# Latent attention in a two-block transformer kernel: units of one head and one query block, and another order of values, first queries and key rotation

## The reference, cut to what matters

```
MLA_HEADS = 8; MLA_NOPE = 64; MLA_ROPE = 32; MLA_SCALE = (64 + 32) ** -0.5; Q_BLOCK = 128

def attention(q_nope, q_rope, k_nope, k_rope, v):
    ...
    def one_block(qs):
        qn, qr = qs
        s = jnp.einsum('bqhd,bkhd->bhqk', qn, k_nope) + jnp.einsum('bqhr,bkr->bhqk', qr, k_rope)
        p = jax.nn.softmax(s.astype(jnp.float32) * MLA_SCALE, axis=-1).astype(v.dtype)
        return jnp.einsum('bhqk,bkhd->bqhd', p, v)
...
k_nope, v = mla_keys_values(kv_c, kv_norm_g, w_ukv)      # kv_c of rank 256
q_nope, q_rope = mla_queries(q_c, q_norm_g, w_uq)        # q_c of rank 384
q_rope = rope_2d(q_rope, ang_row[:, None, :], ang_col[:, None, :])
k_rope = rope_2d(k_rope, ang_row, ang_col)
```

## Time and profile before

| | |
|---|---|
| median of the runs | 3021.17 us |
| the profiled execution | 3019.46 us |
| its span, first to last instruction | 3017.7 us |
| granted TensorE clock, mean over the span | 0.969 of full speed |
| busy share of the span: TensorE, its weight loads | 94%, 75% |
| VectorE, GpSimd, ScalarE | 48%, 38%, 33% |
| DMA read | 364.04 MB, 123 GB/s over the span |

### The profile page before, as it was taken

How to read it: one execution, slowest core, us unless ns; L and a number is a source line. 1 busy time by engine, 2 the same in 40 slices (tenths; PEclk the granted TensorE clock), 3 DMA queues, 4 the chain that set the end, 5 groups by cost and what they waited for, 6 DMA issues and landing times.

```text
span 3017.7 us, 36418 instructions
## 1 busy us (share of the span) xinstructions
PE 2846.8 (94%) x12748; PEld 2261.4 (75%) x12748; DVE 1463.1 (48%) x2627; ACT 997.9 (33%) x1409; POOL 1136.1 (38%) x488
## 2 busy tenths in 40 slices
PE   7999999999999899999899999898788999999997
PEld 4888877778888788887678888787443777788886
DVE  3524365543425534255835253644454365563635
ACT  2222245332322322234532222244333453343322
POOL 2444443234444344443234444453210233344433
PEclk9999999999999999999989999899899999999998
DMA  6535432234436444353215453542100113322221
GB/s 246 209 117 181 147 146 84 79 117 168 154 124 209 138 172 151 140 180 113 70 56 183 142 188 128 193 143 77 70 28 15 56 56 147 112 84 98 97 98 42
DMA packets 69266, 374.32 MB, mean 124 GB/s; under 512 B 7776, under 2 KB 8544, under 8 KB 38656
## 3 DMA queue, kind: packets, MB, share of 16 engines
q1 hardware_dynamic: 65424, 359.61, 33.7%
q10 hardware_dynamic: 3696, 12.85, 1.1%
HBM read 364.04 MB, written 8.39 MB: 123 GB/s over the span
## 4 chain that ended last, share of the span: by engine, by line
PE 39%; issue 33%; POOL 20%; DVE 4%; ACT 2%; DVEq 1%; ACTq 1%; DMA 1%; SPq 1%; POOLq 0%
POOL w_lo L403 20%; PE psum L468 10%; PE psum L470 10%; PE psum L469 10%; PE psum L884 1%; PE psum L862 1%; PE psum L487 1%; PE psum L488 1%; PE psum L489 1%; PE psum L874 1%; DVE psum L1875 1%; PE psum L933 1%; PE psum L935 0%; PE psum L934 0%; SPq L364 0%
## 5 line engine op out<-in xcount | busy, mean ns | idle before, releaser
L403 POOL TENSOR_TENSOR w_lo<-raw,w_hi 128x1024 fp32r<-128x1024 f32 x464 | 1115.0, 2409 | 1723.7 <-ACT w_hi L953 1723.6
L468 PE MATMUL psum<-h_hi,w_hi 128*128 128x512 f32 x2112 | 833.3, 395 | 17.2 <-DVE h_lo L1394 16.6
L469 PE MATMUL psum<-h_lo,w_hi 128*128 128x512 f32 x2112 | 829.1, 393 | 0.0
L470 PE MATMUL psum<-h_hi,w_lo 128*128 128x512 f32 x2112 | 828.3, 392 | 0.0
L953 ACT CAST w_hi<-raw 128x1024 fp32r<-128x1024 f32 x464 | 482.0, 1048 | 913.8 <-PE psum L470 753.6
L468 PEld LDWEIGHTS psum<-h_hi,w_hi 128*128 128x128 f32 x2112 | 401.5, 190 | 106.9 <-DVE h_lo L1394 15.9
L469 PEld LDWEIGHTS psum<-h_lo,w_hi 128*128 128x128 f32 x2112 | 401.5, 190 | 83.8 <-issue 0.5
L470 PEld LDWEIGHTS psum<-h_hi,w_lo 128*128 128x128 f32 x2112 | 400.9, 190 | 84.6
L468 PE MATMUL psum<-hid_hi,w_hi 128*128 128x512 f32 x880 | 349.7, 397 | 4.7 <-DVE hid_lo L1881 4.7
L470 PE MATMUL psum<-hid_hi,w_lo 128*128 128x512 f32 x880 | 349.5, 397 | 0.0
L469 PE MATMUL psum<-hid_lo,w_hi 128*128 128x512 f32 x880 | 349.4, 397 | 0.0
(11 more groups left out here) (343 smaller groups left out, 3067.9 us busy)
## 6 DMA issues: line engine op xcount, KB each, us to landing
raw<-in_weights_dram SPq DMA_DIRECT2D x232, 1024.0 KB, 5.8
mod_raw<-in_mod_w_dram SPq DMA_DIRECT2D x192, 512.0 KB, 4.3
first_mods_a<-in_mod_w_dram SPq DMA_DIRECT2D x8, 512.0 KB, 12.0
first_mods_b<-in_mod_w_dram SPq DMA_DIRECT2D x8, 512.0 KB, 15.4
first_mods_a<-gate_spill ACTq DMA_DIRECT2D x4, 1024.0 KB, 10.9
gate_spill<-gate_out_c ACTq DMA_DIRECT2D x5, 512.0 KB, 3.0
x<-in_xT_dram SPq DMA_DIRECT2D x1, 2048.0 KB, 8.6
x_spill<-x ACTq DMA_DIRECT2D x1, 2048.0 KB, 11.6
```

What stands on the lines that cost most here:

```text
L403: pool.tensor_tensor(w_lo[:, k % 2, cs], raw[:, k % 4, cs], w_hi[:, k % 2, cs].bitcast(F32), ALU.subtract).then_inc(lo_ready, 1)
L468: pe.matmul(out, wh, rhs_hi[:, c, :], start=(c == ks[0]), stop=False)
L469: pe.matmul(out, wh, rhs_lo[:, c, :], start=False, stop=False)
L470: mm = pe.matmul(out, wl, rhs_hi[:, c, :], start=False, stop=(c == ks[-1]))
```

## The change

The attention becomes one loop over 32 units u (head u // 4, query block u % 4). Each unit is turned and multiplied by the values alone: six transposes into banks 4 and 5, two copies on ScalarE into one of two buffers of 768 columns (`turned`: `prod` and a new tile), six matmuls of 128 columns. VectorE scales a unit once its own exponential is there, ahead of the row maximum of the unit after it. On TensorE the order is: turn unit u, scores of unit u + 2, values of unit u - 1. Queries of the next pair are computed after the turn of the pair's seventh unit, keys after that of its eighth; scores of the next pair follow the keys. In the last pair three quarters of block 19 stand in their place. VectorE copies no turned probabilities any more.

In front of the loop: tiles 0 and 1 of the values move ahead of the last context step's state updates; tiles 4 and 5 (in banks 6 and 7), the first queries and tiles 2 and 3 move ahead of the wait for the state chain; the keys follow. Key rotation moves ahead of the last state chain on VectorE, and rotation uses parts of `sq` and `ssq` as scratch.

The added lines of the diff, less eight columns of indentation (where they stand in place of old lines of the functions printed above, those are left out):

```diff
+turned_b, = region([("turned_b", [P, 2 * MOD_COLS], F32)])
...
+turned = [prod[:, :, :].rearrange("p a b -> p (a b)"), turned_b]
...
+vals_ps = sem("vals_ps")
...
+m_turned = sem("m_turned")
+q_ps = sem("q_ps")
...
+    def mla_vals(ts, bank):
+        for i, t in enumerate(ts):
+            for c in range(KV_LORA_C):
+                wh, wl = (w[:, V_K % 2, c * T:(c + 1) * T] for w in (w_hi, w_lo))
+                kh, kl = (k[:, c, t * P:(t + 1) * P] for k in (kvn_hi, kvn_lo))
+                pe.matmul(psum[:, bank + i, :], kh, wh, start=(c == 0), stop=False)
+                pe.matmul(psum[:, bank + i, :], kh, wl, start=False, stop=False)
+                mm = pe.matmul(psum[:, bank + i, :], kl, wh, start=False, stop=(c == 1))
+        mm.then_inc(vals_ps, 1)
...
+        if u == 3:
+            wait_block(G2, V_K)
+            pe.wait_ge(out_free[V_K % 2], 2 * G2 + V_K // 2 + 1)
+            mla_vals((0, 1), 0)
         gla_updates(u, TC)
...
+    def mla_queries(p):
...
+            pe.wait_ge(m_exp, 8 * p - 1 + k % 2)
...
+        pe.wait_ge(out_free[k % 2], 2 * G2 + k // 2 + 1)
+        for t in range(2):
+            out = psum[:, 2 * (k % 2) + t, :]
+            for c in range(Q_LORA_C):
+                wh, wl = (w[:, k % 2, c * 256 + t * P:c * 256 + (t + 1) * P] for w in (w_hi, w_lo))
+                pe.matmul(out, wh, qn_hi[:, c, :], start=(c == 0), stop=False)
+                pe.matmul(out, wh, qn_lo[:, c, :], start=False, stop=False)
+                mm = pe.matmul(out, wl, qn_hi[:, c, :], start=False, stop=(c == Q_LORA_C - 1))
+        mm.then_inc(q_ps, 1)
+    def mla_keys(p):
+        k = PAIR_K + p
+        if p:
+            pe.wait_ge(m_turned, 16 * p)
...
+                if (c, lo) == (KV_LORA_C - 1, 0):
+                    mm.then_inc(front_done, 1)
+        mm.then_inc(block_done, 1)
+    def mla_scores(u):
+        h, qb = u // 4, u % 4
...
+    def mla_turn(u):
+        pe.wait_ge(m_norm, u + 1)
+        if u:
+            pe.wait_ge(m_turned, 2 * u)
...
+            mm = pe.transpose(psum[:, S_BANK + kt // 4, (kt % 4) * P:(kt % 4 + 1) * P], mprobs[:, u % 4, kt * P:(kt + 1) * P],
+                              ident[:, :])
+        mm.then_inc(m_turn, 1)
+    def mla_values(u):
+        h, qb = u // 4, u % 4
+        r, p = 64 * (h % 2), h // 2
+        if u % 8 == 0 and p >= 2:
+            pe.wait_ge(o_mla_ready, p - 1)
+        for kt in range(6):
+            if kt in (0, 4):
+                pe.wait_ge(m_turned, 2 * u + 1 + kt // 4)
+            mm = pe.matmul(psum[r:r + 64, T_BANK + p % 2, qb * P:(qb + 1) * P], vals[:, kt, 64 * h:64 * h + 64],
+                           turned[u % 2][:, kt * P:(kt + 1) * P], start=(kt == 0), stop=(kt == 5))
+        mm.then_inc(m_pv, 1)
+    mla_vals((4, 5), T_BANK)
+    mla_queries(0)
+    pe.wait_ge(vals_ready, 1)
+    mla_vals((2, 3), 0)
+    pe.drain().then_inc(front_done, 1)
+    pe.drain().then_inc(block_done, 1)
+    pe.wait_ge(chain_ready, 8)
+    mla_keys(0)
+    pe.wait_ge(vals_ready, 3)
+    pe.wait_ge(keys_ready, 1)
+    pe.wait_ge(qh_ready, 1)
+    pe.wait_ge(krot_ready, 1)
+    mla_scores(0)
+    mla_scores(1)
+    for u in range(4 * MLA_HEADS):
+        p, j = u // 8, u % 8
+        mla_turn(u)
+        if j < 6:
+            mla_scores(u + 2)
+            if j:
+                mla_values(u - 1)
+        elif j == 6:
+            if p < 3:
+                mla_queries(p + 1)
+            else:
+                pe.wait_ge(m_exp, 32)
+                quarters(G2, GLA_K, (0, 1), hx)
+            mla_values(u - 1)
+        elif p < 3:
+            mla_values(u - 1)
+            mla_keys(p + 1)
+            mla_values(u)
+            pe.wait_ge(keys_ready, p + 2)
+            pe.wait_ge(qh_ready, p + 2)
+            mla_scores(u + 1)
+            mla_scores(u + 2)
+        else:
+            mla_values(u - 1)
+            quarters(G2, GLA_K, (2,), hx)
+            mla_values(u)
+    pe.wait_ge(m_turned, 64)
...
+    quarters(G2, GLA_K, (3,), hx)
+    quarters(G2, GLA_K + 1, range(4), hx)
...
+        act.wait_ge(u_ps[1], 4)
+        for i, (t, bank) in enumerate(((0, 0), (4, T_BANK), (2, 0))):
+            act.wait_ge(vals_ps, i + 1)
+            act.copy(vals[:, t, :], psum[:, bank, :])
+            act.copy(vals[:, t + 1, :], psum[:, bank + 1, :])
+            act.drain().then_inc(vals_ready, 1)
...
+        def take_turned(u):
+            act.wait_ge(m_turn, u + 1)
+            if u >= 2:
+                act.wait_ge(m_pv, u - 1)
+            act.copy(turned[u % 2][:, 0:T], psum[:, S_BANK, :]).then_inc(m_turned, 1)
+            act.copy(turned[u % 2][:, T:TK], psum[:, S_BANK + 1, 0:TC]).then_inc(m_turned, 1)
...
+            act.wait_ge(m_pv, 8 * p + 8)
...
+        def take_keys(p):
+            act.wait_ge(block_done, 4 * G2 + PAIR_K + p + 3)
+            for e in range(2):
+                act.copy(keys[0:64, e, 0:T], psum[64 * e:64 * e + 64, S_BANK, :])
+                act.copy(keys[0:64, e, T:TK], psum[64 * e:64 * e + 64, S_BANK + 1, 0:TC])
+            act.drain().then_inc(keys_ready, 1)
+            split_hi(G2, PAIR_K + p + 2, whole=True)
+        def expo(u):
+            qb, s = u % 4, 2 * (u % 2)
+            act.wait_ge(m_max, u + 1)
+            act.activation(mprobs[:, qb, :], psum[:, s:s + 2, :].rearrange("p a b -> p (a b)")[:, 0:TK], ACT.Exp,
+                           bias=small[:, 0, qb:qb + 1], scale=MLA_SCALE, accum_out=small[:, 1, qb:qb + 1])
+            act.drain().then_inc(m_exp, 1)
+        take_keys(0)
+        expo(0)
+        expo(1)
+        for u in range(4 * MLA_HEADS):
+            p, j = u // 8, u % 8
+            take_turned(u)
+            if j < 6:
+                expo(u + 2)
+            elif j == 7:
+                if p < 3:
+                    take_keys(p + 1)
+                    expo(u + 1)
+                    expo(u + 2)
+                take_out(p)
...
+    def rotate(dst, src, src2):
+        dve.tensor_tensor(sq[64:96, 1, :], src, rot[64:96, :], ALU.mult)
+        dve.tensor_tensor(ssq[64:96, :], src2, rot[96:128, :], ALU.mult)
+        dve.drain()
+        dve.tensor_tensor(dst, sq[64:96, 1, :], ssq[64:96, :], ALU.add)
+        dve.drain()
+    def rotate_keys():
+        dve.wait_ge(rot_landed, 16)
+        for e in range(2):
+            rotate(keys[64:96, e, 0:T], krope[64:96, :], krope[96:128, :])
+        dve.drain().then_inc(krot_ready, 1)
     def gla_context(u):
...
+        if u == 3:
+            rotate_keys()
...
+        def row_max(u):
+            qb, s = u % 4, 2 * (u % 2)
...
+        def normalise(u):
+            qb = u % 4
+            dve.wait_ge(m_exp, u + 1)
+            dve.reciprocal(small[:, 3, qb:qb + 1], small[:, 1, qb:qb + 1])
+            dve.drain()
+            dve.tensor_scalar(mprobs[:, qb, :], mprobs[:, qb, :], small[:, 3, qb:qb + 1], None, ALU.mult).then_inc(m_norm, 1)
+        def take_queries(p):
+            k = PAIR_K + p
+            dve.wait_ge(q_ps, p + 1)
+            for e in range(2):
+                ps = psum[:, 2 * (k % 2) + e, :]
+                dve.tensor_copy(act_ring[0:64, e, :], ps[0:64, :])
+                rotate(act_ring[64:96, e, :], ps[64:96, :], ps[96:128, :])
+            dve.drain().then_inc(out_free[k % 2], 1)
+            dve.drain().then_inc(qh_ready, 1)
+        take_queries(0)
+        row_max(0)
+        row_max(1)
+        normalise(0)
+        for u in range(4 * MLA_HEADS):
+            p, j = u // 8, u % 8
+            if j < 6:
+                normalise(u + 1)
+                row_max(u + 2)
+            elif j == 6:
+                normalise(u + 1)
+                if p < 3:
+                    take_queries(p + 1)
+            elif p < 3:
+                row_max(u + 1)
+                row_max(u + 2)
+                normalise(u + 1)
...
```

More of the change, by code:

```diff
@@ L864, in mla_scores @@
                 mm.then_inc(m_scores, 1)
[L866 to L879, removed]
-                for kt in range(6):
[L881 to L903, removed]
@@ L908, in _ @@
+            pe.wait_ge(m_turned, 64)
             gla_pre(4, krope, T)
-            for j in range(2):
-                products(G2, GLA_K + j, hx)
+            quarters(G2, GLA_K, (3,), hx)
+            quarters(G2, GLA_K + 1, range(4), hx)
             pe.wait_ge(g_in, 1)
@@ L1175, in mla_act @@
                 act.wait_ge(gate_spilled, 16 * 5)
-                act.wait_ge(block_done, 4 * G2 + V_K + 3)
-                for t in range(6):
-                    act.copy(vals[:, t, :], psum[:, t, :])
+                act.wait_ge(u_ps[1], 4)
[4 more added lines that the diff above has]
+                    act.drain().then_inc(vals_ready, 1)
@@ L1218, in mla_act @@
-                for kt in (0, 2, 4):
-                    take_turned(MLA_HEADS - 1, kt)
-                take_out(3)
+                def take_keys(p):
[5 more added lines that the diff above has]
+                    split_hi(G2, PAIR_K + p + 2, whole=True)
@@ L1775, in gla_tokens @@
```

(17 more changed lines are left out.)

92 lines of the change are left out of this document (removed).

## The result

| | before | after |
|---|---|---|
| median of four runs | 3021.49 us | 2984.94 us (2982.52 to 2990.46) |
| the profiled execution, its span | 3019.46, 3017.7 us | 2982.52, 2980.7 us |
| first scores start | 2159.95 us | 2142.31 us |
| gated stage's first block starts | 2363.54 us | 2329.14 us |
| from its start to the end of the span | 654.2 us | 651.6 us |

What follows compares the result with a forecast made beforehand. No engine is full, so the order of work bounds the kernel through TensorE's idle time. Front 17.5 plus loop 30.2 less clock 2.5 gives 45 us off 3021.2: 2976 us, range 2965 to 2999.

Steps and rivals of the forecast that it cites:

- First scores: End of the front: first scores start at 2142.4 us instead of 2159.95, gaining 17.5 us (bounds 14 and 19).
- The unit: Attention loop: one head and 128 queries take 3.52 us on TensorE, which paces the loop.
- changes of shape: TensorE going into or out of products with 64 columns of weights: 0.16 us each, 0.32 per unit.
- Rival (a): Value products in the loop: narrow ones cost per product; gain 29, time 2992 or 2998 us; chance 0.26.
- The ring on VectorE: Loop's cycle of exponential, scaling and row maximum: 3.1 to 3.2 us per unit, under TensorE's 3.52.
- single waits: TensorE before odd query banks' exponentials and first turns after a pair change: 2.4 us in all.
- The pair changes: Three places where the loop's pipeline empties for key copies and first turn: 3.4 us idle each, 10.2 in all.
- first scaling: VectorE ahead of a pair's first turn: 0.9 us within the 5.1 from first scores to first turn.
- The clock: Slow products after gaps at pair changes: 2.5 us taken back from the full-pace gain (bounds 0 and 10).
- The sum: First scores to end of block 20: 170.7 us at full pace instead of 200.9, gaining 30.2.
- block 20: Last block of the attention stretch: expected to end near 2315 us, a sign of the forecast case.
- Rival (b): Clock drops in the loop at shape changes and short waits; all 32 units give 3078 us; chance 0.04 for slower.

Runs made afterwards that it cites:

- e3_maxfirst: Changed kernel with VectorE taking the row maximum of unit u+2 before it scales unit u+1; 3017.48 us, ratio 0.9987 to the kernel before.
- e4_fill: Changed kernel plus 70 unread products, 10 ahead of the first scores and 15 behind each pair's first two scores; 2975.11 us, ratio 0.9848 to the kernel before.
- e5_split: Changed kernel with ScalarE's cast that starts GpSimd's weight split moved behind the turned copies of a pair's seventh unit; 2977.74 us, ratio 0.9841 to the kernel before.

## Why the prediction was right, and where it was short

Point by point, in the prediction's order.

- **First scores.** Forecast 2142.4, measured 2142.31, by the steps named: no idle ahead of updates, values and queries, 2.47 us ahead of the scores for the last key copy. One term was off without a cost: the state chain behind the key rotation started at 2128.17, nearly 1 us later than forecast, since the last addition of that rotation took 2.73 us instead of 0.68 while GpSimd was at work (2.37 us from 2125.10). TensorE had values and queries to do.
- **The unit.** Forecast 3.52, measured 3.56, with narrow products at 0.110 a record for 0.106. The changes of shape, forecast at 0.32, came out at 0.32 too, but spread otherwise: 0.14 around the values, 0.10 on the way from scores to values, and 0.08 between turns and scores, for which the forecast had no term; that they meet the sum is luck. Rival (a) is out.
- **The ring on VectorE** was close to the path as forecast: no turn waits inside a pair, and e3_maxfirst, which puts one maximum of 0.96 us ahead of the scaling, costs 0.66 us in each of sixteen units and more in the second unit of each pair. The "single waits" of 2.4 us hardly appeared.
- **The pair changes.** Forecast 3.4 us idle each, measured 3.85, of which 0.37 ahead of the scores and 3.48 ahead of the first turn. The parts that the forecast names make only 3.0 (1.8 less 1.3, and 2.5); 0.4 of it has no source. The mis-sized part is the first scaling at 0.9 us, which took 1.6 to 2.0 behind GpSimd's split. I had asked only whether the casts on ScalarE end before the next exponential; what the casts start on GpSimd I had not counted. With the start the forecast has about 1.9 us too little.
- **The clock.** This is the term that failed: "I take 2.5 us back". Slow records cost about 1.7 us in the first scores, 3.2 in the first units and 2.6, 1.7 and 1.7 behind the changes (8.67, 8.09 and twice 7.18 less 5.5), together 10.9, just over the upper bound of 10. The sum was made at full pace with its four long idles in plain sight, and the rows of before showed what follows such an idle (10.0 us for four units of scores behind 7.29). e4_fill shows that it was this.
- **The sum.** From the first scores to the gated stage the forecast at full pace has 170.7 + 2.7 = 173.4 us, and 186.8 were measured, 13.4 more: clock 10.9, first scalings 1.9, units 1.1, queries and keys (4.39 and 2.30 for 4.2 and 2.2) 0.9, blocks 19 and 20 0.4, less the single waits 2.4; 0.6 stays unassigned. Charged for the clock were 2.5, so the trace is 10.9 us short of the forecast there; block 20 ended at 2326.5 and not near 2315. The first scores gave 17.6 for 17.5. The median lies only 8.5 us from the forecast, and 2.5 us of that nearness came from the code behind the stage, which nobody had forecast: that is luck.
- **Rival (b)** had the right effect and the wrong place. The clock does not fall through the 64 changes of shape (1.00 in every quiet stretch), nor in e3_maxfirst behind waits of 0.59 us, but behind the few long idles. I had weighed the number of idles, which did fall; what counted was the length of those that stayed.

What stays open: why the same idle costs 2.6 us at one change and 1.7 at another, and why 2.06 us was followed by a slow stretch at the start of e5_split and not at its later changes. The runs show that it happens, not by what rule. Open too is why the clock behind the attention is 0.93 in a stretch of some kernels and 1.00 in others with the same instructions there.

## What to carry to other kernels

Where a pipeline drains, add to the idle what the clock takes behind it: here 3.5 us idle was followed by 1.7 to 2.6 us of lost pace, and the cure was to roll real work of the next stage across the gap, and extra products that nobody reads helped where there was none. Follow a cast to what it starts: an operation on GpSimd next to a VectorE scaling or addition in SBUF on the critical path was a wait here, though both engines are mostly idle. In a ring of exponential, maximum and scaling, the order on VectorE decides; put the operation that TensorE waits for first.

## What the runs showed of the hardware

- Extra products that nobody reads made the kernel 9.8 us faster; 15 of them behind the first two scores of a pair give back the 1.7 to 2.6 us of slow records.
- An idle of 3.48 us was followed by slow records in every change of pair, and one of 2.41 (e5_split) too; one of 2.06 us was not in two changes and was at the start, where the stretch before had held another idle of 2.47. Idles of 0.59 us in every unit of 4.22 (e3_maxfirst) left the records at full pace.
- The scaling of 128x768 in SBUF lasts 0.62 us alone and ends 0.42 us behind GpSimd's product where that is under way.
- Records of 128 columns with 64 columns of weights start 0.110 us apart at full clock; going into them from the scores and coming out of them to the turns costs TensorE some 0.24 us in all (1.38 less 1.28, and 1.46 less 1.32).
